# The first four tiles of the first stage, fed piece by piece: a change to the start of a streaming encoder step

## The reference, cut to what matters

```
def rms_norm(x, g):
    y = xf * rsqrt(mean(xf * xf, axis=-1) + EPS)
    return y * g
def macaron_half(x, g, w_in, w_out):
    a, b = split(rms_norm(x, g) @ w_in, 2, axis=-1)
    return x + 0.5 * ((silu(a) * b) @ w_out)
```

## Time and profile before

| | us |
|---|---|
| median of 3 runs | 1280.23 (1280.08 to 1280.53) |
| profiled execution | 1280.21 |
| its span | 1278.4 |
| PE busy in the span | 1265.4 |
| matmul groups L490, L491, L492 of this form | 545.8, 543.0, 543.0 |

### The profile page before, as it was taken

How to read it: one execution, slowest core, us unless ns; L and a number is a source line. 1 busy time by engine, 2 the same in 40 slices (tenths; PEclk the granted TensorE clock), 3 DMA queues, 4 the chain that set the end, 5 groups by cost and what they waited for, 6 DMA issues and landing times.

```text
span 1278.4 us, 22446 instructions
## 1 busy us (share of the span) xinstructions
PE 1265.4 (99%) x8784; PEld 1243.9 (97%) x8784; DVE 741.6 (58%) x1128; ACT 561.2 (44%) x827; POOL 174.8 (14%) x208
## 2 busy tenths in 40 slices
PE   9999999999999999999999999999999999999999
PEld 8999999999998999999999999999997899999999
DVE  7756574555677656554454675554446756656433
ACT  7534363353275533333343453433345763343322
POOL 0300020046143100000122000000124510000000
PEclk9999999999999999999999999999999999999999
DMA  8454445553203444444443533454451144343443
GB/s 279 163 160 150 161 139 174 195 188 132 100 34 130 164 151 145 160 163 139 151 164 123 196 133 138 157 164 160 135 187 34 55 144 159 137 164 131 135 140 128
DMA packets 39661, 187.45 MB, mean 147 GB/s; under 512 B 4369, under 2 KB 14353, under 8 KB 24497
## 3 DMA queue, kind: packets, MB, share of 16 engines
q1 hardware_dynamic: 38272, 183.38, 41.8%
q0 software_dynamic: 1184, 3.13, 1.1%
q10 hardware_dynamic: 144, 0.11, 0.0%
HBM read 179.70 MB, written 6.90 MB: 146 GB/s over the span
## 4 chain that ended last, share of the span: by engine, by line
PE 95%; DVE 2%; ACT 1%; issue 1%; DMA 1%; SPq 0%; ACTq 0%; DVEq 0%
PE bank L490 29%; PE bank L492 29%; PE bank L491 29%; PE bank L752 1%; PE bank L713 1%; PE bank L890 1%; PE bank L755 1%; PE bank L722 1%; DVE wlo L1526 1%; DMA raw<-in_w_ffn_in 1%; ACT whi L1120 0%; PE outs L516 0%; ACT ew L1281 0%; PE outs L518 0%; PE outs L500 0%
## 5 line engine op out<-in xcount | busy, mean ns | idle before, releaser
L490 PE MATMUL bank<-xhi,whi 128*128 128x320 f32 (+1 forms) x1760 | 545.8, 310 | 3.0 <-DVE wlo L1901 1.1
L492 PE MATMUL bank<-xhi,wlo 128*128 128x320 f32 (+1 forms) x1760 | 543.0, 309 | 0.0
L491 PE MATMUL bank<-xlo,whi 128*128 128x320 f32 (+1 forms) x1760 | 543.0, 309 | 0.0
L1526 DVE TENSOR_TENSOR wlo<-raw,whi 128x2048 fp32r<-128x2048 f32 (+1 forms) x177 | 364.1, 2057 | 230.2 <-ACT whi L1120 230.1
L1120 ACT ACTIVATE whi<-raw 128x2048 fp32r<-128x2048 f32 (+1 forms) x177 | 304.1, 1718 | 242.3 <-PE bank L492 237.9
L490 PEld LDWEIGHTS bank<-xhi,whi 128*128 128x128 f32 x1760 | 330.5, 188 | 6.2 <-issue 3.4
L491 PEld LDWEIGHTS bank<-xlo,whi 128*128 128x128 f32 x1760 | 330.6, 188 | 0.5
L492 PEld LDWEIGHTS bank<-xhi,wlo 128*128 128x128 f32 x1760 | 330.5, 188 | 0.0
L490 PE MATMUL bank<-hhi,whi 128*128 128x320 f32 x704 | 219.0, 311 | 0.0
L492 PE MATMUL bank<-hhi,wlo 128*128 128x320 f32 x704 | 217.5, 309 | 0.0
L491 PE MATMUL bank<-hlo,whi 128*128 128x320 f32 x704 | 217.5, 309 | 0.0
(11 more groups left out here) (233 smaller groups left out, 1041.5 us busy)
## 6 DMA issues: line engine op xcount, KB each, us to landing
raw<-in_w_ffn_in SPq DMA_DIRECT2D x86, 1024.0 KB, 4.8
raw<-in_w_ffn_out SPq DMA_DIRECT2D x64, 704.0 KB, 4.2
raw<-in_w_in_a SPq DMA_DIRECT2D x10, 1024.0 KB, 4.8
raw<-in_w_out SPq DMA_DIRECT2D x8, 1024.0 KB, 4.9
raw<-in_w_kv SPq DMA_DIRECT2D x6, 1024.0 KB, 4.8
raw<-in_w_mkv SPq DMA_DIRECT2D x4, 1024.0 KB, 4.7
raw<-in_w_in_b SPq DMA_DIRECT2D x4, 1024.0 KB, 4.7
raw<-in_w_ffn_in SPq DMA_DIRECT2D x8, 256.0 KB, 7.2
```

Of the source, the lines that this page charges most:

```text
L490: mm(acc, wh, mhi(ks[q]), start=start and q == 0, stop=False)
L491: mm(acc, wh, mlo(ks[q]), start=False, stop=False)
L492: last = mm(acc, wl, mhi(ks[q]), start=False, stop=stop and q == nk - 1)
L1526: tt(wlo[slot][:, 0:size], raw[slot][:, 0:size], f32(whi[slot][:, 0:size]), ALU.subtract).then_inc(lo_ready[slot], 1)
```

## The change

The diff, cut to its core:

- `START` cuts the eight pieces `k` into five groups: 1, 1, 2, 2 and 2. For each group SP starts `x`, the part of the first block and the part of the second block (the second block's first part is started by ACT, behind `early`).
- PE takes each group for all four tiles before the next; the norm's matmul stands before the last group of slot 1. Only 15 matmuls on zeroed data come ahead.
- ACT and DVE split group by group for both slots; the eight squares and the seven additions come behind all of it.
- The third block is loaded by halves: the first one as soon as three groups of the first block are split, the second when the first block is wholly split. ACT splits the first half when PE is through the first half of the first block. Both halves of the third block's split, and the whole split of the fourth block, now stand ahead of `body(0)` on DVE and ahead of the stage's loop on ACT; DVE does the second half ahead of its part of the norm, and ACT too.
- The first two tiles of pair 1 go to `banks[4]` and `banks[5]` without a wait for a free bank; the small product of `biases` goes to `HS`.
- POOL's constants wait for the third block's second half.

```diff
+START = [(0, 1), (1, 2), (2, 4), (4, 6), (6, 8)]
+LAST = len(START) - 1
@@ sync
+            for q, (k0, k1) in enumerate(START):
+                own = slice(256 * k0, 256 * k1)
+                sp.dma_start(x[:, k0:k1], x_v[:, k0:k1]).then_inc(d_x[q], 16)
+                sp.dma_start(raw[0][:, own], weights["in0"][0][:, own]
+                             ).then_inc(d_piece[q] if q < LAST else landed[0], 16)
+                if q:
+                    sp.dma_start(raw[1][:, own], weights["in0"][1][:, own]
+                                 ).then_inc(d_piece1[q] if q < LAST else landed[1], 16)
+            sp.wait_ge(piece_lo, 3)
+            sp.dma_start(raw[0][:, 0:BLK // 2], weights["in0"][2][:, 0:BLK // 2]).then_inc(d_third, 16)
+            sp.wait_ge(lo_ready[0], 1)
+            sp.dma_start(raw[0][:, BLK // 2:BLK], weights["in0"][2][:, BLK // 2:BLK]).then_inc(landed[0], 16)
+            sp.wait_ge(lo_ready[1], 1)
+            sp.dma_start(raw[1][:], weights["in0"][3]).then_inc(landed[1], 16)
@@ tensor, first_pieces
+                    for q, (k0, k1) in enumerate(START):
+                        pe.wait_ge(xn_lo, k1)
+                        for slot, some in ((0, piece_lo), (1, piece1_lo)):
+                            if q == LAST:
+                                pe.wait_ge(lo_ready[slot], 1)
+                                if slot == 1:
+                                    row_norm(stage, R)
+                            else:
+                                pe.wait_ge(some, q + 1)
...
+                            if slot == 0 and k1 == KD // 2:
+                                last.then_inc(first_half, 1)
@@ tensor, body
-                        wait_acc(t0 + 4 * i + j)
+                        spare = halves and j < 2
+                        if not spare:
+                            wait_acc(t0 + 4 * i + j)
-                        product(banks[j][:, 0:R], slot, col, 256, range(KD), KD,
+                        product(banks[4 + j if spare else j][:, 0:R], slot, col, 256, range(KD), KD,
@@ tensor
-            for _ in range(19):
+            for _ in range(15):
@@ scalar
+            act.dma_start(raw[1][:, 0:256], weights["in0"][1][:, 0:256]).then_inc(d_piece1[0], 16)
...
+            for k in range(KD):
+                nc.scalar.activation(sq8[:, k, :], x[:, k, :], ACT.Square).then_inc(sq_ready, 1)
+            act.wait_ge(d_third, 16)
+            act.wait_ge(first_half, 1)
+            nc.scalar.activation(whi[0][:, 0:BLK // 2], raw[0][:, 0:BLK // 2], ACT.Copy).then_inc(third_hi, 1)
             act.wait_ge(landed[0], 16 * (PAIR0["in0"] + 1) + 16)
             act.wait_ge(acc_ready, TILE0["in0"] + 2)
+            nc.scalar.activation(whi[0][:, BLK // 2:BLK], raw[0][:, BLK // 2:BLK], ACT.Copy).then_inc(hi_ready[0], 1)
             row_norm("in0", R)
+            split_hi(1, PAIR0["in0"] + 1, BLK, acc_ready, TILE0["in0"] + 4)
@@ vector
...
             tt(wlo[0][:, 0:BLK // 2], raw[0][:, 0:BLK // 2], f32(whi[0][:, 0:BLK // 2]), ALU.subtract
                ).then_inc(third_lo, 1)
+            dve.wait_ge(hi_ready[0], PAIR0["in0"] + 2)
+            tt(wlo[0][:, BLK // 2:BLK], raw[0][:, BLK // 2:BLK], f32(whi[0][:, BLK // 2:BLK]), ALU.subtract
+               ).then_inc(lo_ready[0], 1)
             row_norm("in0", R)
+            split_lo(1, PAIR0["in0"] + 1, BLK)
@@ gpsimd
-            pool.wait_ge(landed[1], 16)
+            pool.wait_ge(landed[0], 32)
```

More of the change, by code:

```diff
@@ L1212, in body @@
                     for c in range(2):
-                        if c == 1:
+                        if c == 1 and not (stage == "in0" and isinstance(i, int) and i == 0):
                             split_hi(1, n0 + i + 1, BLK if size is None else size, acc_ready, t0 + 4 * i + 4)
@@ L1403, in _ @@
                     input_hi(x[:, k, :], xhi[:, k, :], "ffn1_0", k)
[L1404 to L1410, removed]
@@ L1412, in piece1 @@
-            def piece1(q):
-                act.wait_ge(d_piece1[q] if q < 3 else landed[1], 16)
-                nc.scalar.activation(whi[1][:, 512 * q:512 * (q + 1)], raw[1][:, 512 * q:512 * (q + 1)], ACT.Copy
-                                     ).then_inc(piece1_hi if q < 3 else hi_ready[1], 1)
-            piece1(0)
-            squares(range(4))
-            piece1(1)
-            squares(range(4, KD))
-            piece1(2)
-            piece1(3)
+                act.wait_ge(d_piece[q] if q < LAST else landed[0], 16)
@@ L1640, in body @@
                 def body(i, size, at=None):
+                    spare = stage == "in0" and isinstance(i, int) and i == 1
                     for c in range(2):
                         dve.wait_ge(acc_ready, t0 + 4 * i + c + 1)
-                        tt(gate[:, c, :], banks[c][:, 0:R], r[:], ALU.mult).then_inc(acc_free, 1)
+                        tt(gate[:, c, :], banks[4 + c if spare else c][:, 0:R], r[:], ALU.mult).then_inc(acc_free, 1)
                         if at:
@@ L1663, in ffn_in @@
                     for i in range(3):
-                        body(i, BLK, third if stage == "in0" and i == 0 else None)
+                        body(i, BLK)
                         after(i)
@@ L1894, in _ @@
             nc.vector.memset(f32(lf8_lo[:]), 0.0)
-            for q in range(4):
-                inputs_lo("in0", "ffn1_0", lambda k: x[:, k, :], R, tiles=(2 * q, 2 * q + 1))
-                if q < 3:
+            for q, (k0, k1) in enumerate(START):
+                own = slice(256 * k0, 256 * k1)
+                inputs_lo("in0", "ffn1_0", lambda k: x[:, k, :], R, tiles=range(k0, k1))
+                if q < LAST:
                     dve.wait_ge(piece_hi, q + 1)
```

78 lines of the change are left out of this document (28 added, 50 removed).

## The result

The changed kernel takes 1284.85 us (median of 6 runs, 1284.27 to 1287.05); beside it the kernel before took 1280.21 (1280.00 to 1282.44). That is 4.6 us slower, and outside the forecast range. The profiled execution took 1284.45, its span 1282.4, 4.0 more than before.

The account below looks back on a forecast made before the run. PE bounds the kernel, but ACT and DVE must feed pair 2: PE's 0.9 us lead at tile 3 is outweighed by 2.3 us more waiting there, so 1280.23 + 1.4 = 1281.6 us; own range 1280.8 to 1282.5, 8-in-10 range 1278.6 to 1283.2.

Parts of the forecast that it names:

- PE's start: First products start 1.6 us sooner, at 5.6; one stop of 1.9 before the third group; first four tiles end 0.9 sooner.
- The fourth block: Its whole split ahead of body(0) idles DVE some 1.1 us; wlo begins at 24.9, the first gate near 27.2.
- the whole sum: Net change at pair 2's start: 40.3 instead of 38.91, +1.4 us, with nothing behind it giving it back; chance 0.55.
- Unknown costs: Transfer effects: small pieces taken as 0, fourth block's landing 0 to +0.3, constants' later start 0 with ends 0 and +1.
- the line: ACT's and DVE's chain of passes up to pair 2's weights, forecast to end at 40.2, with PE starting at 40.3.
- rival 4: Kernel start: with 15 zeroed matmuls the clock rises later, 0.12 us per slow product, 2.4 for 36, to 1284.0; chance 0.05.
- Rival 3: First six pieces: small transfers at half the rate, +2.7 us on every landing behind, to 1284.3; chance 0.1.
- Rival 1: Start: input lands 1 us sooner, additions end at 19.1, pair 2 starts about 0.1 sooner than before, 1280.1; chance 0.2.
- Rival 2: Wait at pair 2 stays covered as ACT and DVE catch up; PE's 0.9 and the old 0.6 count, 1278.7; chance 0.1.

Follow-up runs that it names:

- e4: e1 with the fourth block's whole split put back into body(0) on ACT and DVE; 1283.45 against 1279.61 us for the kernel before, ratio 1.0026.
- e1: Changed kernel with POOL starting the constants' transfers when the second block has landed, as in the old kernel; 1286.71 against 1279.61 us, ratio 1.0047.
- h2: h1 with the fourth block's whole split put back into body(0) on ACT and DVE; 1281.06 against 1279.14 us for the kernel before, ratio 1.0014.
- h1: Changed kernel with ACT's wait ahead of hhi set to the early constants instead of POOL's five; 1282.56 against 1279.14 us, ratio 1.0023.
- g1: Changed kernel with the memory rows' 1 MB transfer moved behind the load of slot 0 for pair 2; 1285.81 against 1279.41 us, ratio 1.0050.
- i1: The changed kernel run again, unedited; 1285.94 against 1279.40 us for the kernel before, ratio 1.0048.
- e3: Old kernel with POOL starting the constants only when the third block has landed; 1280.87 against 1279.61 us, ratio 1.0010.
- g2: g1 with the memory rows' passes spread behind body(1) and body(2), their squares one and two pairs later; 1282.02 against 1279.41 us, ratio 1.0021.
- h3: h1 with memory rows' passes spread, squares later, PE's biases product behind tile 7, POOL's scratch stores held back; 1278.95 against 1279.14 us, ratio 0.9998.
- g3: Old kernel with the memory rows' passes spread as in g2; 1280.76 against 1279.41 us, ratio 1.0008.
- h4: g3 (old kernel, memory rows' passes spread) with POOL's scratch stores held back; 1278.45 against 1279.14 us, ratio 0.9993.
- g4: e1 with 24 matmuls on zeroed data on PE behind tile 7, inside its wait for pair 2; 1285.33 against 1279.41 us, ratio 1.0049.
- i2: Changed kernel with 20 matmuls on zeroed data on PE behind tile 7, inside its wait for pair 2; 1284.30 against 1279.40 us, ratio 1.0039.

## Why the prediction was wrong, step by step

- **PE's start: right.** 5.41 for 5.6; the third group at 11.02 for 11.3; stop 1.74 for 1.9; norm at 20.36 for 20.1, where PE waited 0.31 for the additions; 0.55 ahead at the end of the first four tiles for 0.9.
- **The fourth block: right.** `wlo` at 25.34 for 24.9, the takes at 27.55 for 27.2. Put back into `body(0)`, the split lets pair 2 start 1.46 sooner in e4 than in e1, and 1.96 sooner in h2 than in h1; so the new place costs about what I had for the whole sum, 1.4.
- **The step that failed** is the one in "Unknown costs" that put the constants' later start at 0, "with the ends 0 and +1". I took their last landing from the start of their issues and not from what is in front of them. The first issue is at 20.68 (19.4 taken), the last ends 3 us later, and its data is 8 us behind, as the fourth block, the memory rows and pair 2's load share the engines (with the memory rows' transfer moved behind, in g1, it landed 6.5 after its issue instead of 8.2). ACT asked at 28.9 and waited 2.32 (2.31 in i1); 1.8 of it moves the line, as `hid` is ready at 29.4 only. h1's edit takes away this wait and nothing else, and all its runs lie below all those of the changed kernel; h1 is 3.4 above the kernel before, the changed kernel 4.6 and, in i1, 6.5. e3 makes the same wait in the old kernel. With it the sum is 1.4 + 1.8 = 3.2, and 3.66 was measured at pair 2; the 0.5 left is lateness of the line itself, seen in h1's profile as 40.78 for the forecast 40.3, most of it (0.35) there by the first `gate`. That 1.4 and the full wait of 2.3 also add up to 3.7 is chance.
- **The clock, rival 4: a right price per product, and mostly another place.** I gave it 0.05 and put it on the first products. In the first profile the products after 15 matmuls ran at 0.147 at once. But the late rise that I described is in the profiles of e1, g1 and h1 (4 to 11 of the first products at 0.267, hidden, since PE would have waited for the third group anyway), and in g2 and h3 the clock fell behind that stop (1.89 in h3), 11 or 12 products that nothing hides. It is in none of the four profiles with the old start (before, e3, g3, h4). In the changed kernel's own profiles the lower level came behind two other stops: 1.28 for the constants, and the one before pair 2. The first is hidden, the second is not. It is in some executions and not in others: the changed kernel's median is 0.6 above its fastest run (1284.27, granted clock 1.000), and i1's is 1.8 above. g4's and i2's profiles, with PE kept busy, have no stretch behind the wait for pair 2.
- **Rival 3, small pieces: did not happen.** ACT's split of the last piece ended at 15.32 (forecast 15.4). By the estimate from the Trainium skill's page "DMA: Bandwidth & Descriptors", section "Bandwidth", 138 GB/s at 64 KB, it would have ended 3.4 us later; the trace does not agree, as the pieces of 128 to 320 KB moved 319 GB/s between 3 and 6 us (the old order: 329). From 6 to 9 us they moved 212 where the old order moved 297, so they were not free, but no stop on the line came out longer than forecast. That page's section "Issuing engines are not separate DMA queues" says that transfers of SP, ACT and POOL interleave on the same DMA engines; e1 agrees: beside POOL's 970 KB, ACT could take SP's 512 KB at 23.13 instead of 20.39.
- **Rival 1, the input comes sooner: did not happen.** The additions ended at 20.21 (forecast 20.1; 19.1 for this rival).
- **Rival 2, the gain is there if the wait at pair 2 stays covered: not found.** In h3 it is covered, and the time lies between 1.4 below and 0.9 above the old kernel's; beside h4, which has the old start, it is 0.5 higher, which the intervals do not part. So the new start by itself gave nothing that can be measured here.
- Of the 4.24 between the two profiled executions, 3.66 is at pair 2, 0.34 comes up to the span's end (DVE's first `x` tile behind the first attention block is 3.91 late), and 0.24 is outside the span. The last two I did not look into.

## What to carry to other kernels

Before you reorder the start of a kernel, write down every transfer in flight around it with its size, and who waits for each; a transfer that is issued 6 us later lands later still when others have been put in front of it, and an earlier issue of it delays those others. Take the landing as a range: `lamv` was there at 31.2 in one execution and at 27.6 in another with the same transfers, so check in each profile that what an edit takes away would have been there. Count of a wait only what is left when the next one behind it takes over: 2.32 of waiting was worth 1.8. A head start of the busiest engine is worth only what the engines that feed it also gain; follow the line to the next block's last wait and sum that. And count a stop of a matmul engine twice where it may be followed by slower products.

## What the runs showed of the hardware that was not expected

- Behind single stops of 1.3 to 4.3 us in a dense run of matmuls the granted clock fell to its lower level (products by 0.267 instead of 0.147): 13 products after the stop of 1.28, 13 more in i1 after 1.77, 18 in e1 after 4.31. After the shorter ones it fell when PE was at work again (stop until 31.21, fall at about 32.4); in e1 it fell within the stop, at about 41.7. It did not fall behind 1.78 in the first profile or 1.39 in e4.
- One 512 KB transfer issued at 15.55, ahead of two of 1 MB issued at 16.15 and 16.52, took 4.8 us to land; with 970 KB more from another queue, 7.3. Without the second of 1 MB it took 5.5 (g1).
- Six small stores to memory sent within 3.5 us were followed by a 1 MB load that came 5.95 us late, and by a stop of PE of 1.83 us, 20 us after the first of them; spaced out by 7 us and more, there was no such stop.
